# The router's products in two column groups of TensorE, with the logits copied out and turned back

## What is computed

```python
xl = xl + gt1 * ol                                    # ol = mixer output @ w_o + b_o
hl = modulate(rmsnorm(xl, norm_g[i, 1]), sh2, sc2)    # x * (1 + scale) + shift
...
glog = (xt @ w_group + b_group).astype(jnp.float32)   # 4 group logits
_, g_sel = lax.top_k(glog, 1)
elog = (jnp.einsum('nd,gde->nge', xt, w_expert) + b_expert[None]).astype(jnp.float32)   # 32 expert logits
e_val, e_idx = lax.top_k(elog_g, TOP_K)
weights = g_w * jax.nn.softmax(e_val, axis=-1)
```

## Time and profile before

| what | value |
|---|---|
| median of 3 runs | 2783.92 us (2781.77 to 2784.31) |
| the profiled execution | 2781.91 us, span of its core 2780.0 us |
| TensorE, matmuls busy | 2589.4 us, 93% of the span |
| VectorE busy | 1244.1 us, 45% |
| ScalarE busy | 707.4 us, 25% |
| GpSimd busy | 473.3 us, 17% |
| L1052, the router's records | 288, 37.2 us busy |

### The profile page before, as it was taken

How to read it: one execution, slowest core, us unless ns; L and a number is a source line. 1 busy time by engine, 2 the same in 40 slices (tenths; PEclk the granted TensorE clock), 3 DMA queues, 4 the chain that set the end, 5 groups by cost and what they waited for, 6 DMA issues and landing times. The chain is left out here.

```text
span 2780.0 us, 68755 instructions
## 1 busy us (share of the span) xinstructions
PE 2589.4 (93%) x28310; PEld 1804.0 (65%) x28311; DVE 1244.1 (45%) x2852; ACT 707.4 (25%) x1479; POOL 473.3 (17%) x590
## 2 busy tenths in 40 slices
PE   7999999999989959999999689999999499999995
PEld 6888788878745537777777484555544376677773
DVE  3234333433455632222222266557566355555555
ACT  3222222222321003333333365334410000000002
POOL 0112111111121112222222220000011122222223
PEclk9999999999999969999999899999999699999998
DMA  6322233132345288999999840010233899999996
GB/s 262 121 97 100 97 105 135 62 117 85 115 154 190 105 338 317 415 416 396 415 416 416 292 160 31 21 41 30 100 129 136 336 374 416 416 416 416 416 410 254
DMA packets 128717, 644.33 MB, mean 232 GB/s; under 512 B 18912, under 2 KB 31616, under 8 KB 72656
## 3 DMA queue, kind: packets, MB, share of 16 engines
q1 hardware_dynamic: 94960, 539.66, 49.1%
q0 software_dynamic: 17984, 57.16, 5.6%
q10 hardware_dynamic: 15648, 45.71, 4.2%
HBM read 577.89 MB, written 64.57 MB: 231 GB/s over the span
## 5 line engine op out<-in xcount | busy, mean ns | idle before, releaser
L1690 PE MATMUL PS<-wt,xT 128*32 128x256 f32 x13056 | 750.5, 381 | 39.3 <-DVE xT L1819 26.3
L1690 PEld LDWEIGHTS PS<-wt,xT 128*32 128x32 f32 x13056 | 505.9, 110 | 244.7 <-issue 48.8
L1705 PE MATMUL PS<-wt,hidT 128*32 128x256 f32 x6528 | 396.3, 380 | 4.1 <-DVE y L1840 2.4
L1705 PEld LDWEIGHTS PS<-wt,hidT 128*32 128x32 f32 x6528 | 254.6, 110 | 103.2 <-issue 5.8
L1819 DVE STREAM_TRANSPOSE xT<-xg 128x256 f32<-128x256 f32 x206 | 91.8, 445 | 493.6 <-PE PS L1690 477.7
L720 PE MATMUL PS<-hT,slab 128*128 128x256 f32 x1280 | 296.3, 386 | 6.3 <-DVE low L613 3.5
L720 PEld LDWEIGHTS PS<-hT,slab 128*128 128x128 f32 x1280 | 240.3, 192 | 42.7 <-issue 6.5
L1619 ACT ACTIVATE u<-PS 128x128 f32<-128x128 f32 x206 | 57.1, 277 | 754.7 <-PE PS L1690 745.1
L433 POOL TENSOR_SCALAR prob<-prob,inv 128x640 f32<-128x640 f32 (+2 forms) x80 | 130.1, 1626 | 662.8 <-DVE inv L628 662.8
L1586 POOL DMA_INDIRECT xg<-h_d,ib x212 | 207.6, 979 | 166.8 <-POOL ib L1583 166.0
L1627 ACT ACTIVATE y<-PS 32x256 f32<-32x256 f32 x416 | 155.8, 375 | 155.3 <-PE PS L1705 151.6
(11 more groups left out here) (254 smaller groups left out, 2772.3 us busy)
## 6 DMA issues: line engine op xcount, KB each, us to landing
wt<-in_w SPq DMA_DIRECT2D x256, 1024.0 KB, 10.8
wt<-in_w2s SPq DMA_DIRECT2D x128, 1024.0 KB
aw<-in_ada_w SPq DMA_DIRECT2D x48, 1024.0 KB, 5.0
ys_d<-y ACTq DMA_DIRECT2D x204, 128.0 KB
slab<-in_slabs SPq DMA_DIRECT2D x24, 512.0 KB, 3.4
tab<-in_tables SPq DMA_DIRECT2D x8, 1408.0 KB, 7.3
ys_d<-zero POOLq DMA_DIRECT2D x4, 2560.0 KB, 9.6
x_d<-x_p ACTq DMA_DIRECT2D x18, 512.0 KB, 4.9
```

The costliest lines, as they stand in the source:

```text
L1690: mm = t.matmul(PS[32 * g:32 * g + 32, UP, 0:QD], xT[:, k * 32:k * 32 + 32], wt[b][:, q, c * 1024 + g * QD:c * 1024 + g * QD + QD], start= ...
L1705: mm = t.matmul(PS[32 * g:32 * g + 32, DOWN, 0:QD], hT_[:, k * 32:k * 32 + 32], wt[b][:, q, c * 1024 + g * QD:c * 1024 + g * QD + QD], sta ...
```

## The change

The router's weights become the stationary operand and the turned tile the moving one. Product k goes to column group k % 2: output partitions 0 to 35 for even k, 64 to 99 for odd k, of the PSUM bank beside the old one. This gives two partial sums of the logits, turned (logits x tokens). ScalarE copies both to `lt`, a 128 x 128 tile whose other rows are zero; a new product (`logits_back`) multiplies `lt` by `both`, a 128 x 36 matrix of two stacked identities, which adds the halves and turns them back to 128 tokens x 36 in the old bank. VectorE reads them there as before. `both` and the zeros of `lt` are made once in each projection on VectorE. On TensorE logits_back(n - 1) stands behind part(n + 1, 0), and for tile 1 directly behind route(1).

```diff
--- before.py
+++ after.py
@@ -818,6 +818,7 @@
                 self.wr, self.rbias = tensor("wr", [P, KD, NR]), tensor("rbias", [P, NR])
                 self.ss, self.rt = tensor("ss", [P, 2]), tensor("rt", [P, 2])
                 self.bo = tensor("bo", [P, D])
+                self.lt, self.both = tensor("lt", [P, P]), tensor("both", [P, NR])
                 put.at = LATE_AT
                 self.gt, self.ng = tensor("gt", [P, self.W, D]), tensor("ng", [P, D])
                 self.g, self.sh = tensor("g", [P, self.W, D]), tensor("sh", [P, self.W, D])
@@ -834,6 +835,7 @@
                     nm(x) for x in ("product", "x1", "rows_made", "biased"))
                 self.sum_ok, self.sqrt_ok, self.norm_ok, self.h_ok = (
                     nm(x) for x in ("sum", "sqrt", "normed", "h"))
+                self.HALF = [slice(64 * c, 64 * c + NR) for c in range(2)]
                 self.tr_ok, self.ev_ok, self.rt_ok, self.rl_ok, self.ch = (
                     nm(x) for x in ("turned", "copied", "router", "logits", "choice"))
 
@@ -903,9 +905,10 @@
                     a.wait_ge(self.h_ok, n + 1)
                     a.dma_start(h2_d[rows, :], self.hb[j][:, :]).then_inc(self.h_out[j], 16)
                     a.wait_ge(self.tr_ok, n + 1)
-                    if n:
-                        a.wait_ge(self.rt_ok, n)
                     a.activation(flat(self.ht[:, :, :]), banks(4, 2), ACT.Copy).then_inc(self.ev_ok, 1)
+                    a.wait_ge(self.rt_ok, 2 * n + 1)
+                    for rows in self.HALF:
+                        a.activation(self.lt[rows, :], PS[rows, self.route_at + 1, 0:P], ACT.Copy).then_inc(self.ev_ok, 1)
                 for j in range(2):
                     a.wait_ge(self.x_out[j], 8 * self.nt)
                     a.wait_ge(self.h_out[j], 8 * self.nt)
@@ -961,7 +964,7 @@
                     v.tensor_tensor(self.hb[j][:, :], self.hb[j][:, :], self.sh[:, w, :], ALU.add).then_inc(self.h_ok, 1)
 
                 def logits(n):
-                    v.wait_ge(self.rt_ok, n + 1)
+                    v.wait_ge(self.rt_ok, 2 * n + 2)
                     v.tensor_tensor(RLs[:, n, :], PS[:, self.route_at, 0:NR], self.rbias[:, :], ALU.add).then_inc(self.rl_ok, 1)
 
                 def choose(lo, hi):
@@ -1006,6 +1009,8 @@
                     added(n)
                     if n == 0:
                         v.wait_ge(self.wr_in, 16 * (W + 2))
+                        link(v.memset(self.lt[:, :], 0.0))
+                        link(v.tensor_tensor(self.both[:, :], ident[:, self.HALF[0]], ident[:, self.HALF[1]], ALU.add))
                         link(v.memset(A2[:, nt, :], 0.0))
                         link(v.memset(A2c[:, 0, :], 0.0))
                     elif n == 2:
@@ -1037,20 +1042,25 @@
             def turn(self, t, n):
                 t.wait_ge(self.h_ok, n + 1)
                 if n:
-                    t.wait_ge(self.ev_ok, n)
+                    t.wait_ge(self.ev_ok, 3 * n - 2)
                 for k in range(KD):
                     mm = t.transpose(banks(4, 2)[:, k * P:(k + 1) * P], self.hb[n % 2][:, k * P:(k + 1) * P], ident[:, :])
                 mm.then_inc(self.tr_ok, 1)
 
             def route(self, t, n):
-                t.wait_ge(self.ev_ok, n + 1)
+                t.wait_ge(self.ev_ok, 3 * n + 1)
                 if n == 0:
                     t.wait_ge(self.wr_in, 16 * (self.W + 2))
-                else:
+                for k in range(KD):
+                    mm = t.matmul(PS[self.HALF[k % 2], self.route_at + 1, 0:P], self.wr[:, k, :], self.ht[:, k, :],
+                                  start=(k < 2), stop=(k >= KD - 2))
+                mm.then_inc(self.rt_ok, 1)
+
+            def logits_back(self, t, n):
+                t.wait_ge(self.ev_ok, 3 * n + 3)
+                if n:
                     t.wait_ge(self.rl_ok, n)
-                for k in range(KD):
-                    mm = t.matmul(PS[:, self.route_at, 0:NR], self.ht[:, k, :], self.wr[:, k, :], start=(k == 0), stop=(k == KD - 1))
-                mm.then_inc(self.rt_ok, 1)
+                t.matmul(PS[:, self.route_at, 0:NR], self.lt[:, :], self.both[:, :], start=True, stop=True).then_inc(self.rt_ok, 1)
 
             def rest(self, t):
                 H = KD // 2
@@ -1059,18 +1069,21 @@
                 self.part(t, 2, 1, 0, H)
                 self.route(t, 0)
                 self.part(t, 2, 1, H, KD)
+                self.logits_back(t, 0)
                 self.turn(t, 1)
                 self.part(t, 3, 0, 0, KD)
                 self.route(t, 1)
                 for n in range(2, self.nt):
                     if n > 2 and n + 1 < self.nt:
                         self.part(t, n + 1, 0, 0, KD)
+                    self.logits_back(t, n - 1)
                     if n + 1 < self.nt:
                         self.part(t, n + 1, 1, 0, H)
                     self.turn(t, n)
                     if n + 1 < self.nt:
                         self.part(t, n + 1, 1, H, KD)
                     self.route(t, n)
+                self.logits_back(t, self.nt - 1)
```

## The result

| what | before | changed kernel |
|---|---|---|
| median of 20 runs each | 2784.15 us | 2788.97 us |
| ratio to before | | 1.0016, 95% interval 1.0009 to 1.0023 |
| the profiled execution's span | 2780.0 | 2788.4 |
| TensorE, matmuls busy | 2589.4 | 2584.9 |
| ScalarE busy | 707.4 | 717.1 |

One of the changed kernel's 20 runs took 6976.53 us, for a reason that nothing here shows: the median counts it (without it 2788.96), the ratio doesn't.

What follows compares the result with a forecast made beforehand. TensorE was taken to bound mid-stage projections, VectorE's chain their two ends. Steady -2.6, first tiles +3.1, +0.6 and +0.2, last +2.1 sum to +3.4 us on 2783.9: 2787, range 2781 to 2794.

Steps and rivals of the forecast that it cites:

- Route: TensorE, router product of one tile: 1.14 us instead of 1.70, so -0.56 each; bounds 0.88 and 1.97.
- Product back: TensorE, the one added matmul of 2 records: +0.21 us each where TensorE is busy; bounds 0.1 and 0.6.
- bound of 1.97: TensorE, route time if the two column groups take turns; as rival 2 it gave 2802 us, chance 0.06.
- Steady sum: Mid-stage tiles of both projections: routes -6.7, products back +2.1, collisions with GpSimd's add +2.0, together -2.6 us.
- Spare of the turn: VectorE's normed rows in mid-stage: of 5.5 us of spare before the turn that wants them, 0.2 is left.
- rival 1: Mid-stage: product back reaches VectorE 0.4 us later, spare gone, 10 turns late, +4.0 to 2791.3 us; chance 0.17.
- GpSimd's add: Mid-stage, VectorE's multiplication by the gain held up by GpSimd's add: +0.1 to +0.5 us for each of 8 tiles, +2.0 together.
- First tiles: Turn(1) late through ScalarE's queue and GpSimd's add: +2.0 us first projection, +1.1 second; bounds together -0.2 and +4.5.
- step between route(1) and its product back: TensorE waits through the route's tail and ScalarE's copies at tile 1: +0.3 us each projection, +0.6 for both.
- VectorE's two instructions: Memset and add before the first reciprocal: +0.2 us for both projections together; bounds 0 and 0.4 in each.
- Last tiles: Each projection's end: gate behind the choice of experts +1.42 us, last route -0.37, together +1.05, times two +2.1.
- the lock: VectorE beside GpSimd's add: released 2.22 us after the add's start; the skill's whole-instruction rule would make the term +3.0.

Runs made afterwards that it cites:

- one-group kernel: The changed kernel with all eight products of a route in column group 0, both copies kept; 2798.98 us in one run.
- late logits: The changed kernel with VectorE reading the logits of tile n - 1 behind the normed rows of tile n; 2785.16 us, ratio to before 0.9999.
- add held back: The changed kernel with GpSimd's add for tile n + 2 also waiting until tile n's normed rows are ready; 2785.78 us in its one execution.
- two repeats: The changed kernel as it is, profiled twice more; first projection 148.32 and 148.73 us.
- Sqrt edit: The changed kernel with ScalarE copying the two halves of tile n only after the Sqrt of tile n + 1; 2788.84 us, ratio to before 1.0012.

## Why the prediction was right

I forecast 2787, +3.4 us against before, within 2781 to 2794; measured is 2788.97, +4.5 by the ratio. The mechanisms that it named were there, and in the changed kernel no turn in mid-stage waited over 1 us. The number came out near partly by luck, as the terms show:

- **Route**: 1.14 forecast, 1.10 measured. **Product back**: 0.21 forecast, 0.26 measured, because the gap of 0.12 ahead of it counts too. Together a period without waits is 16.03 where it was 16.39: -0.36 for the forecast -0.35. The bound of 1.97 for groups that take turns is what the one-group kernel showed.
- **Steady sum**: -6.7 + 2.1 = -4.6 counted 12 routes and 10 products back. Between turn(2) and the turn before the last lie only 10 routes in the two projections together, and with the late logits, where nothing waits, that stretch is shorter by 2.18 + 1.46 = 3.6. The other two, routes 8 and 6, follow the last product, where TensorE waits 4.71 for VectorE in any case: with the late logits turn(8) to turn(9) is 10.89 as before, though the route is cheaper. These 2 x 0.56 = 1.1 were not on the path.
- **Spare of the turn**: forecast 0.2 left of 5.5. With the add held back, the rows of tile 3 were ready at 881.15 and their turn started at 881.62, in its slot: 0.47 left, of which the step from VectorE to TensorE takes 0.05. So 0.4, twice the forecast, and rival 1's 0.4 would just about have used it up.
- **GpSimd's add**: 0.1 to 0.5 each, +2.0 over 8 tiles. The three executions of the changed kernel had, over 16.03 in the five periods of projection 0, 2.2, 0.9 and 1.3, and in the three of projection 1 0.2 to 0.4. The mechanism is right and the size is 1.1 to 2.4; it differs from run to run with the landing of the load of x, which I had only from one execution. In the profiled execution of the result it was 2.4. One wait of 0.97 (17.00) was beyond the 0.5 that I gave as the most.
- **First tiles**: in projection 0 forecast +2.0, measured +1.74 (turn(1) at 852.79 for the forecast 852, in an execution whose turn(0) was 1.06 later than before). In projection 1 forecast +1.1, measured +0.22 here, +0.06 and -0.05 in the two repeats. Here route(0) came 7.25 behind turn(0) for 6.65, in products mostly at half clock, and TensorE was no earlier than the rows. In the repeats route(0) came 5.90 and 6.66 behind turn(0), and turn(1) did wait, 1.18 and 0.31. In the second repeat, with route(0) placed as before (6.66), the rows were ready 11.8 behind turn(0), where the forecast has 12.2 to 13.6 (2065.0 to 2066.4 less 2052.80): GpSimd's add began 7.1 behind turn(0), where it was 8.9 and the forecast allowed for 1.3 less, so that it was nearly over when L961 came and stretched it by 0.3 only. This term was too large by 0.9. The step between route(1) and its product back: +0.3 forecast, +0.42 measured in each projection; the two copies, 0.27 each and 0.30 apart, take 0.57, at the upper end of my 0.45 to 0.6, and the product back its 0.26. VectorE's two instructions: +0.2 forecast, 0.3 in projection 1 and nothing in projection 0.
- **The clock**: missing. I carried the pause of 2.0 as its own price only; what follows it can cost 1.7 more. It brought the sum of the profiled execution to 4.7 + 0.3 + 0.3 = 5.3 instead of 3.6. Of three executions of the changed kernel all had it, and of the unprofiled runs no row tells.
- **Last tiles**: +1.42 for the gate behind the choice, measured 12.08 - 10.89 = +1.19; -0.37 for the last route, measured 12.75 - 13.15 = -0.40. The cold route (at half clock) lasted 1.93 for the 2.03 worked out. With both projections this term is 1.6 for 2.1.

The forecast's 3.4 and the profiled execution's 5.3 differ by 1.9. The gain that was not on the path (+1.0), the adds (+0.5), the step behind route(1) (+0.2) and the clock (+1.7) stand, with 0.1 for VectorE's two instructions, against the first tiles (-1.1) and the last ones (-0.5). Without the clock it would be 3.6 for 3.4, and that is luck: errors of about 1 us on either side cancelled. The +4.5 of the medians lies between, and the other stages' own variation of some us is in it.

On the lock, the prediction weighed the Trainium skill's rule (SBUF — State Buffer, Who interferes with whom) that the second instruction is blocked for the whole of the first. The changed kernel's tile 4 has L961 released at 899.76 - 1.28 = 898.48, 0.20 before the add's recorded end 898.68 and 2.14 behind its start. The trace thus agrees but for these 0.20, and is nearer to the 2.22 that the forecast took from its rows. And it works both ways, as that page has it: at 849.06 GpSimd's add came second, 0.39 before the end of L961, and lasted 2.60 for 2.35.

## What to carry to other kernels

A product that is made cheaper by two more steps (copy out, product back) has a longer latency even where it costs less engine time: list who reads its result, and what is queued behind that reader, before counting the gain. Here the reader stood ahead of work it had nothing to do with, on VectorE and on ScalarE. Moving the reader behind that work on VectorE took the loss of 0.16% to nothing (ratio 0.9999), and with the copies behind the Sqrt and half a part in front of one product back it became 0.21% faster. An engine that is pushed later by some us meets other engines: look at what starts in the window that it is moved into. And when such queue edits come in pairs, try them together: the Sqrt edit alone made a new wait that the logits edit took away.

## What the runs showed of the hardware that I had not expected

A pause of 2 us on TensorE in the middle of dense products was sometimes followed, in or right behind the turn that ends it, by some 3.5 us of mostly half clock and sometimes not, with the same instructions: 4 of 10 executions, 1.69 us each. Shorter pauses were never followed by a fall: those of 0.67 us between route(1) and its product back, those of 1.02 to 1.04 us ahead of turn(0) in projection 0 (route(0) 4.4 to 4.5 behind it each time), and those of 0.21 to 1.18 us ahead of turn(1) in projection 1 (turn(1) to turn(2) 13.38 or 13.39 there in the changed kernel's executions). The Trainium skill (TensorE: Matmul & The Clock Gate, What's actually happening) says that the chip's windows run free of the kernel; the two executions of one kernel that differ agree with it.
